# Opening loads in halves with the constants last, and low parts one step later in the selecting attention

## The chip, the cores and the metric

The kernel runs on one core of one Trainium2 chip. The metric is the device time of an execution in microseconds (us), lower is better. Engines: PE (TensorE, matrix products), DVE (VectorE), ACT (ScalarE), POOL (GpSimd), SP (SyncE, here only a DMA queue).

## The reference, cut to what matters

Two transformer-like blocks over 512 tokens of width 1024, all in float32. The first block runs twice (two layers), the second once. Each layer begins with `h = rms_norm(x, g)` and a wide projection `z = h @ w_in`. The first block then mixes multi-head latent attention, a two-dimensional Fourier transform of `h` (`fourier_mix`) and windowed attention; rotary angles come from `positions`. The second block mixes a linear recurrence, a pooling branch and a *selecting* attention (`dsa_attention`: an index score picks 128 keys per query out of up to 512, and eight heads attend to those alone); later it attends to a memory of 256 vectors, whose keys and values (`m @ w_kv`) are independent of the tokens.

## The kernel before, in words

**Operands in two parts.** Each float32 operand of a matrix product is split into a rounded high part (`hi`, written by ACT as fp32r) and the remainder (`lo = value - hi`, by DVE or POOL). A product takes three matmuls: hi·hi, hi·lo, lo·hi (lines 672 to 677).

**The weight stream.** All weights lie in one tensor `stream` in the order of their use, cut into units of 128 x 2048 floats (1 MiB, 16 blocks of 128 x 128). SP loads unit v into `raw[v % 2]` (line 650 for unit 0, 654 for unit 1, 658 for all others) as soon as the low part of unit v-2 is done (semaphore `lo_ready`). ACT writes `w_hi` once PE has finished with the unit two before (`split_unit`, line 1315); DVE writes `w_lo` (line 1953; by halves in `split_piece`, line 2177), which counts up `lo_ready`; PE waits for it before the first block of a unit.

**The start (layer 0).** SP issues unit 0, then x in four transfers of 512 KB (two of eight row groups each), then unit 1. ACT's queue issues the gain vector `g_in`, `pos_i` (positions) and `cst_sb` (identity, ones, masks, frequencies). ACT splits unit 0 (line 1647), then for each of the eight row groups m of x writes `raw_x_hi[m]` (1651) and its square (1652). DVE writes `w_lo[0]` (2420) and then the eight `raw_x_lo[m]` (2424), adds up the squares (2428, 2429), and splits units 2 and 3 (1953). PE (`begin`) takes unit 0 over k = 0..7, six matmuls of 512 columns for each k, then unit 1. Within unit 1, at n = 0 and k = 5, it sums the squares over the partitions (`begun_sum`, line 800, against the ones in `cst_sb`); from this ACT makes the reciprocal root, DVE the normed x (`res`, lines 2023 and 2447), ACT its high part `h_hi` (1367), and POOL its low part `h_lo` (2782).

**POOL's order.** POOL waits for `pos_loaded` and `cst_loaded`, runs `turns()` (lines 2870 to 2879: thirteen instructions, a cast, nine tensor_scalar, three tensor_tensor, each waiting for the one before), which makes the reduced rotary angles `cs`, and only behind them the eight `h_lo` of the layer. Nothing reads `cs` before some 70 us. The Fourier stage `four1`, which follows `begin` on PE, waits for `h_lo` of k = 0 and 1 before its first tile.

**The selecting attention** (`attention(c, "dsa", ...)`). 32 items t (a head and a block of 128 queries). DVE, in step t: the masked minimum of the scores of item t (2199, "reduce", counts `shift_ready`); at t = 11, 19, 27 the low part of a finished output (`output_lo`, 2229); reciprocal and scaling of item t-1 (2212, 2214); then `evac_mem(t)`, which holds the low parts of the weight units. PE, in step t: for even t the score matmuls of t and t+1 (883), which wait for the reduce of t-1; the transposes of item t-3 (908); the value products (957); then two blocks of the memory's keys (up to t = 15) or one of its values (t = 16 to 31). ACT's steps hold exponentials (1510), copies (1499) and, at fixed t, the `w_hi` of units. The unit whose low part is written at t = 5 and 6 ("am"'s last split) is the second of the memory's keys; PE needs it in step 8.

Of the kernel before, what the change touches and what calls it, by code (L numbers as in the profile page):

```python
# [14 lines left out]
P = 128  # L15
# [248 lines left out]
def block_kernel(nc, stream, xT, pT, memT, vec1, gains, cst, pos, out):  # L264
    with ExitStack() as ctx:
        def sem(name):
            return ctx.enter_context(nc.semaphore(name))
# [151 lines left out]

        def home(c, v):  # L420

            block = 1 if c.base is BASE1 else 2
            wrapped = block == 1 and v >= TOTAL1["U"]
            if wrapped:
                v -= TOTAL1["U"]
            if block == 1 and c.layer == 0 and v < 2 and not wrapped:
                return second if v == 1 else (w_hi[0], w_lo[0])
            for (b, st), two in EARLY.items():
                u = v - c.base[st]["U"] if b == block else -1
                if 0 <= u < 2 and two[u] is not None:  # L430
                    return two[u]
            return w_hi[v % 2], w_lo[v % 2]
# [27 lines left out]
        tile_free = sem("tile_free")  # L460
        x_loaded = [sem(f"x_loaded{i}") for i in range(4)]
# [186 lines left out]
        @block.sync  # L648
        def _(sp):
            sp.dma_start(raw[0][:, :], stream[0]).then_inc(raw_ready[0], 16)  # L650
            for i in range(4):
                k = slice(2 * i, 2 * i + 2)
                sp.dma_start(x[:, k, :], xT.rearrange("(k p) s -> p k s", p=P)[:, k, :]).then_inc(x_loaded[i], 16)
            sp.dma_start(raw[1][:, :], stream[1]).then_inc(raw_ready[1], 16)
            with sp.Fori(1, UNITS_PADDED // 2) as i:
                for p in range(2):
                    sp.wait_ge(lo_ready, i * 2 + (p - 1))
                    sp.dma_start(raw[p][:, :], stream[bass.ds(i * 2 + p, 1)].rearrange("a p n -> (a p) n")).then_inc(raw_ready[p], 16)
            for p in range(2):
                sp.wait_ge(raw_ready[p], 16 * (UNITS_PADDED // 2))  # L660
# [3 lines left out]
        def _(pe):  # L664
# [159 lines left out]
            def begin(c, st, turn):  # L824

                u0 = c.base[st]["U"]
                if turn == 0:
                    pe.wait_ge(lo_ready, c.at("U", st, 1))
                    hi, lo = home(c, u0)
                    two = [free_bank(c, st, n) for n in range(2)]  # L830
                    for k in range(KD):
                        pe.wait_ge(raw_split, c.begun("W", 2 * k + 2))
# [7 lines left out]
                    for n in range(2):  # L840
                        ps = free_bank(c, st, 2 + n)
                        for k in range(KD):
                            b = slice((8 * n + k) * P, (8 * n + k + 1) * P)
                            mm = mac_at(ps[:, :], hi[:, b], lo[:, b], raw_x_hi[:, k, :], raw_x_lo[:, k, :], k == 0, k == KD - 1)
                            if n == 0 and k == 5:
                                begun_sum(c, 0, 0)
                                begun_sum(c, 1, 0)
# [442 lines left out]
        def _(act):  # L1290
# [353 lines left out]
            act.dma_start(pos_i[:, :], pos).then_inc(pos_loaded, 16)  # L1644
            act.dma_start(cst_sb[:, :], cst).then_inc(cst_loaded, 16)
            act.wait_ge(raw_ready[0], 16)
            nc.scalar.activation(w_hi[0][:, :], raw[0][:, :], ACT.Copy).then_inc(hi_ready, 1)
            act.wait_ge(gain_loaded, 16)
            for m in range(KD):
                act.wait_ge(x_loaded[m // 2], 16)  # L1650
                nc.scalar.activation(raw_x_hi[:, m, :], x[:, m, :], ACT.Identity, scale=g_in[:, m:m + 1]).then_inc(raw_hi, 2)
                nc.scalar.activation(sq_x[:, m, :], x[:, m, :], ACT.Square).then_inc(x_squared, 1)
            act.wait_ge(raw_ready[1], 16)
            nc.scalar.activation(second[0][:, :], raw[1][:, :], ACT.Copy).then_inc(hi_ready, 1)
            log_table()
# [277 lines left out]
        def _(dve):  # L1933
# [487 lines left out]
            first_low(0, w_hi[0], w_lo[0])  # L2421
            for m in range(KD):
                dve.wait_ge(raw_hi, 2 * m + 2)
# [326 lines left out]
            def evac_mem(t):  # L2750
                if t in (5, 6):
                    split_piece(c, "am", SPLIT_LATER["am"], t - 5)
                after_blocks(c, "mk", t, 2, lambda n: None)
                if t in (25, 33):
                    split_unit(c, "mv", (t - 25) // 8)
# [443 lines left out]
```

## Time and profile before

| | us |
|---|---|
| median of 3 runs | 2708.15 (2705.16 to 2709.49) |
| the profiled execution | 2703.69 |
| its span, first to last instruction | 2701.7 |

The profiled execution is 2.0 us longer than its span, and 4.5 us below the median. A change of about 0.2% (5.4 us) can be told from none. The page gives, by engine, the busy share; by line, count, duration and the idle time ahead. A busy PE counts matmuls whose ends are modelled, so only its idle gaps and its rate tell something.

### The profile page before, as it was taken

How to read it: one execution, taken by the hardware profiler on the slowest of the kernel's cores; microseconds unless marked ns; L12 is line 12 of the kernel's file. 1: busy time of each engine (PE TensorE's matmuls, PEld its weight loads, DVE VectorE, ACT ScalarE, POOL GpSimd, SP SyncE). 2: the span in 40 equal slices, each digit the busy share in tenths (PEclk: the TensorE clock that was granted, in tenths of full speed). 3: DMA queues.
4: the chain of work that ended last, by engine and by line, in shares of the span. 5: the costliest groups of instructions: out<-in, count | busy, mean ns of one | idle time of the engine just before them, and what ended most of it. 6: DMA issues, size and time to landing. Idle time of an engine off the chain costs nothing. (4 is left out here: it accounts for less than half of the span.)

```text
span 2701.7 us, 40494 instructions
## 1 busy us (share of the span) xinstructions
PE 2633.5 (97%) x15788; PEld 2264.9 (84%) x15788; DVE 1711.3 (63%) x2738; ACT 1303.0 (48%) x2274; POOL 558.3 (21%) x556
## 2 busy tenths in 40 slices
PE   8999999999999999999999999999999999999997
PEld 6887778999888988777899998897787688899976
DVE  6667544888624765754388862466688537698733
ACT  6446543555524643654355552463634535555521
POOL 5124001210402312400121031241001012210131
PEclk9999999999999999999999999999999999999999
DMA  4321123222332232111222232222232222123332
GB/s 151 125 94 40 48 78 110 78 93 96 110 109 97 85 116 94 48 56 63 101 87 94 102 118 94 95 94 94 78 123 80 79 94 79 48 94 107 106 112 83
DMA packets 37558, 246.55 MB, mean 91 GB/s; under 512 B 4608, under 2 KB 5632, under 8 KB 8448
## 3 DMA queue, kind: packets, MB, share of 16 engines
q1 hardware_dynamic: 33632, 239.09, 24.9%
q10 hardware_dynamic: 3744, 4.94, 0.5%
q8 instruction: 126, 2.06, 0.3%
q14 instruction: 56, 0.46, 0.1%
HBM read 241.91 MB, written 2.10 MB: 90 GB/s over the span
## 5 line engine op out<-in xcount | busy, mean ns | idle before, releaser
L1953 DVE TENSOR_TENSOR w_lo<-raw,w_hi 128x2048 fp32r<-128x2048 f32 x130 | 305.4, 2351 | 320.3 <-ACT w_hi L1315 319.8
L675 PE MATMUL bank<-h_hi,w_hi 128*128 128x512 f32 (+1 forms) x1224 | 472.3, 386 | 3.2 <-DVE ob_lo L2464 1.3
L677 PE MATMUL bank<-h_hi,w_lo 128*128 128x512 f32 (+1 forms) x1224 | 463.7, 379 | 0.0
L676 PE MATMUL bank<-h_lo,w_hi 128*128 128x512 f32 (+1 forms) x1224 | 463.3, 378 | 0.0
L1315 ACT ACTIVATE w_hi<-raw 128x2048 fp32r<-128x2048 f32 x151 | 288.1, 1910 | 240.0 <-PE bank L677 231.3
L1065 PE MATMUL bank<-half_hi,w_hi 128*128 128x256 f32 x1344 | 380.5, 283 | 0.0
L1066 PE MATMUL bank<-half_lo,w_hi 128*128 128x256 f32 x1344 | 380.4, 283 | 0.0
L1067 PE MATMUL bank<-half_hi,w_lo 128*128 128x256 f32 x1344 | 380.3, 283 | 0.0
L675 PEld LDWEIGHTS bank<-h_hi,w_hi 128*128 128x128 f32 x1224 | 230.3, 188 | 55.4 <-issue 11.5
L677 PEld LDWEIGHTS bank<-h_hi,w_lo 128*128 128x128 f32 x1224 | 230.2, 188 | 44.2
L676 PEld LDWEIGHTS bank<-h_lo,w_hi 128*128 128x128 f32 x1224 | 230.6, 188 | 39.7
L1065 PEld LDWEIGHTS bank<-half_hi,w_hi 128*128 128x128 f32 x1344 | 257.9, 192 | 0.3
L1066 PEld LDWEIGHTS bank<-half_lo,w_hi 128*128 128x128 f32 x1344 | 258.0, 192 | 0.1
L1067 PEld LDWEIGHTS bank<-half_hi,w_lo 128*128 128x128 f32 x1344 | 258.0, 192 | 0.0
L675 PE MATMUL bank<-a_hi,w_hi 128*128 128x512 f32 x528 | 206.8, 392 | 6.6 <-POOL a_lo L2809 5.8
L676 PE MATMUL bank<-a_lo,w_hi 128*128 128x512 f32 x528 | 206.2, 390 | 0.0
L677 PE MATMUL bank<-a_hi,w_lo 128*128 128x512 f32 x528 | 206.0, 390 | 0.0
L2300 DVE TENSOR_TENSOR w_lo<-raw,w_hi 128x512 fp32r<-128x512 f32 x192 | 141.0, 736 | 32.6 <-ACT w_hi L1558 31.4
L1499 ACT ACTIVATE pT<-bank 128x512 f32<-128x512 f32 (+3 forms) x168 | 83.0, 494 | 127.6 <-PE bank L908 125.1
L1558 ACT ACTIVATE w_hi<-raw 128x512 fp32r<-128x512 f32 x192 | 118.7, 623 | 18.0 <-PE bank L1067 9.7
L675 PEld LDWEIGHTS bank<-a_hi,w_hi 128*128 128x128 f32 x528 | 99.4, 188 | 29.1 <-POOL a_lo L2809 7.0
L2782 POOL TENSOR_TENSOR m_lo<-res,m_hi 128x512 fp32r<-128x512 f32 x24 | 31.1, 1294 | 436.8 <-ACT m_hi L1367 436.8
(508 smaller groups left out, 5802.9 us busy)
## 6 DMA issues: line engine op xcount, KB each, us to landing
raw<-in_stream SPq DMA_DIRECT2D x226, 1024.0 KB, 4.8
x<-in_xT SPq DMA_DIRECT2D x4, 512.0 KB, 8.7
out_T<-x ACTq DMA_DIRECT2D x8, 256.0 KB, 2.0
p_f<-in_pT ACTq DMA_DIRECT2D x2, 512.0 KB, 3.6
memf<-in_memT ACTq DMA_DIRECT2D x1, 1024.0 KB, 5.4
cst_sb<-in_cst ACTq DMA_DIRECT2D x1, 409.0 KB, 7.3
pos_i<-in_pos ACTq DMA_DIRECT2D x1, 258.0 KB, 6.1
g_in<-in_gains ACTq DMA_DIRECT2D x3, 4.0 KB, 3.5
```

What stands on the lines that cost most here:

```text
L675: nc.tensor.matmul(ps, wh, xh, start=start, stop=False)
L676: nc.tensor.matmul(ps, wh, xl, start=False, stop=False)
L677: return nc.tensor.matmul(ps, wl, xh, start=False, stop=stop)
L1065: nc.tensor.matmul(ps, wh[:, b], half_hi[:, i, k, :], start=opens, stop=False, skip_group_check=on)
L1066: nc.tensor.matmul(ps, wh[:, b], half_lo[:, i, k, :], start=False, stop=False, skip_group_check=on)
L1067: mm = nc.tensor.matmul(ps, wl[:, b], half_hi[:, i, k, :], start=False, stop=k == KD // 2 - 1, skip_group_check=on)
L1315: nc.scalar.activation(home(c, v)[0][:, :], raw[v % 2][:, :], ACT.Copy).then_inc(hi_ready, 1)
L1499: nc.scalar.activation(a["pT"][h % 2][:, 0:n, b * P:(b + 1) * P], TURNED[:, 0:n * P].rearrange("p (t q) -> p t q", t=n), ACT.Copy).then_in ...
L1558: ins = nc.scalar.activation(factor(c, v, i, w_hi), factor_value(c, v, i), ACT.Copy)
L1953: nc.vector.tensor_tensor(lo[:, :], raw[v % 2][:, :], hi[:, :].bitcast(F32), ALU.subtract).then_inc(lo_ready, 1)
L2300: ins = nc.vector.tensor_tensor(factor(c, v, i, w_lo), factor_value(c, v, i), factor(c, v, i, w_hi).bitcast(F32), ALU.subtract)
L2782: nc.gpsimd.tensor_tensor(dst, src, hi.bitcast(F32), ALU.subtract).then_inc(res_split, 1)
```

## The change

Four edits at the start and one in the selecting attention:

- Unit 0 comes in two halves by k (k = 0..3 and 4..7 of both of its column tiles, pieces of 2 KB in a row): half 0, x's first transfer, half 1, x's other three, unit 1. `cst` and `pos` move from ACT's queue to the end of SP's opening list, behind unit 1.
- ACT and DVE split half 0 first, then m = 0 of x, then half 1; PE waits for half 0 only and for `lo_ready` at k = 4. The squares of x come one or more steps later on ACT, the last four behind unit 1's high part.
- The sum of squares moves on PE from k = 5 to k = 7 of unit 1's first tile.
- In the selecting attention DVE writes the low parts in halves at t = 6, 7 (was 5, 6), 10, 11 and 18, 19 (were 9, 10 and 17, 18), 26, 27 and 33, 34 (were whole units at 25 and 33). ACT's and PE's orders there stay.

```diff
@@ -417,6 +417,10 @@
             (2, "gu"): [early("gu2_0", 0, 8), early("gu2_1", 16, 24)],
         }
 
+        def of_front(w, half):
+
+            return w.rearrange("p (n k c) -> p n (k c)", n=2, k=KD)[:, :, half * (KD // 2) * P:(half + 1) * (KD // 2) * P]
+
         def home(c, v):
 
             block = 1 if c.base is BASE1 else 2
@@ -458,6 +462,9 @@
         part_done = sem("part_done")
         act_took = sem("act_took")
         tile_free = sem("tile_free")
+        front_loaded = sem("front_loaded")
+        front_hi = sem("front_hi")
+        front_split = sem("front_split")
         x_loaded = [sem(f"x_loaded{i}") for i in range(4)]
         gain_loaded = sem("gain_loaded")
         post_ready = sem("post_ready")
@@ -647,11 +654,15 @@
 
         @block.sync
         def _(sp):
-            sp.dma_start(raw[0][:, :], stream[0]).then_inc(raw_ready[0], 16)
+            sp.dma_start(of_front(raw[0], 0), of_front(stream[0], 0)).then_inc(front_loaded, 16)
             for i in range(4):
                 k = slice(2 * i, 2 * i + 2)
                 sp.dma_start(x[:, k, :], xT.rearrange("(k p) s -> p k s", p=P)[:, k, :]).then_inc(x_loaded[i], 16)
+                if i == 0:
+                    sp.dma_start(of_front(raw[0], 1), of_front(stream[0], 1)).then_inc(raw_ready[0], 16)
             sp.dma_start(raw[1][:, :], stream[1]).then_inc(raw_ready[1], 16)
+            sp.dma_start(cst_sb[:, :], cst).then_inc(cst_loaded, 16)
+            sp.dma_start(pos_i[:, :], pos).then_inc(pos_loaded, 16)
             with sp.Fori(1, UNITS_PADDED // 2) as i:
                 for p in range(2):
                     sp.wait_ge(lo_ready, i * 2 + (p - 1))
@@ -825,10 +836,12 @@
 
                 u0 = c.base[st]["U"]
                 if turn == 0:
-                    pe.wait_ge(lo_ready, c.at("U", st, 1))
+                    pe.wait_ge(front_split, 1)
                     hi, lo = home(c, u0)
                     two = [free_bank(c, st, n) for n in range(2)]
                     for k in range(KD):
+                        if k == KD // 2:
+                            pe.wait_ge(lo_ready, c.at("U", st, 1))
                         pe.wait_ge(raw_split, c.begun("W", 2 * k + 2))
                         for n in range(2):
                             b = slice((8 * n + k) * P, (8 * n + k + 1) * P)
@@ -842,7 +855,7 @@
                         for k in range(KD):
                             b = slice((8 * n + k) * P, (8 * n + k + 1) * P)
                             mm = mac_at(ps[:, :], hi[:, b], lo[:, b], raw_x_hi[:, k, :], raw_x_lo[:, k, :], k == 0, k == KD - 1)
-                            if n == 0 and k == 5:
+                            if n == 0 and k == 7:
                                 begun_sum(c, 0, 0)
                                 begun_sum(c, 1, 0)
                         mm.then_inc(tile_done, 1)
@@ -1641,17 +1654,24 @@
                 act.dma_start(g_in[:, :], gains[bass.ds(row, 1)].rearrange("a p n -> (a p) n")).then_inc(gain_loaded, 16)
 
             act.dma_start(g_in[:, :], gains[0]).then_inc(gain_loaded, 16)
-            act.dma_start(pos_i[:, :], pos).then_inc(pos_loaded, 16)
-            act.dma_start(cst_sb[:, :], cst).then_inc(cst_loaded, 16)
-            act.wait_ge(raw_ready[0], 16)
-            nc.scalar.activation(w_hi[0][:, :], raw[0][:, :], ACT.Copy).then_inc(hi_ready, 1)
+            act.wait_ge(front_loaded, 16)
+            nc.scalar.activation(of_front(w_hi[0], 0), of_front(raw[0], 0), ACT.Copy).then_inc(front_hi, 1)
             act.wait_ge(gain_loaded, 16)
+
+            def square_x(m):
+                nc.scalar.activation(sq_x[:, m, :], x[:, m, :], ACT.Square).then_inc(x_squared, 1)
             for m in range(KD):
                 act.wait_ge(x_loaded[m // 2], 16)
                 nc.scalar.activation(raw_x_hi[:, m, :], x[:, m, :], ACT.Identity, scale=g_in[:, m:m + 1]).then_inc(raw_hi, 2)
-                nc.scalar.activation(sq_x[:, m, :], x[:, m, :], ACT.Square).then_inc(x_squared, 1)
+                if m == 0:
+                    act.wait_ge(raw_ready[0], 16)
+                    nc.scalar.activation(of_front(w_hi[0], 1), of_front(raw[0], 1), ACT.Copy).then_inc(hi_ready, 1)
+                elif m <= 4:
+                    square_x(m - 1)
             act.wait_ge(raw_ready[1], 16)
             nc.scalar.activation(second[0][:, :], raw[1][:, :], ACT.Copy).then_inc(hi_ready, 1)
+            for m in range(4, KD):
+                square_x(m)
             log_table()
             act.wait_ge(tile_done, Counts(BASE1, 0).at("T", "z1a", 2))
             for u in range(2):
@@ -2418,8 +2438,12 @@
             def first_low(v, hi, lo):
                 dve.wait_ge(hi_ready, v + 1)
                 nc.vector.tensor_tensor(lo[:, :], raw[v][:, :], hi[:, :].bitcast(F32), ALU.subtract).then_inc(lo_ready, 1)
-            first_low(0, w_hi[0], w_lo[0])
+            dve.wait_ge(front_hi, 1)
+            nc.vector.tensor_tensor(of_front(w_lo[0], 0), of_front(raw[0], 0), of_front(w_hi[0], 0).bitcast(F32), ALU.subtract).then_inc(front_split, 1)
             for m in range(KD):
+                if m == 1:
+                    dve.wait_ge(hi_ready, 1)
+                    nc.vector.tensor_tensor(of_front(w_lo[0], 1), of_front(raw[0], 1), of_front(w_hi[0], 1).bitcast(F32), ALU.subtract).then_inc(lo_ready, 1)
                 dve.wait_ge(raw_hi, 2 * m + 2)
                 nc.vector.scalar_tensor_tensor(out=raw_x_lo[:, m, :], in0=x[:, m, :], scalar=g_in[:, m:m + 1],
                                                in1=raw_x_hi[:, m, :].bitcast(F32), op0=ALU.mult, op1=ALU.subtract).then_inc(raw_split, 2)
@@ -2748,11 +2772,14 @@
             dve.wait_ge(res_ready, result_value(c, "normm", KD - 1))
 
             def evac_mem(t):
-                if t in (5, 6):
-                    split_piece(c, "am", SPLIT_LATER["am"], t - 5)
-                after_blocks(c, "mk", t, 2, lambda n: None)
-                if t in (25, 33):
-                    split_unit(c, "mv", (t - 25) // 8)
+                if t in (6, 7):
+                    split_piece(c, "am", SPLIT_LATER["am"], t - 6)
+                for u in range(2):
+                    if t in (8 * u + 10, 8 * u + 11):
+                        split_piece(c, "mk", u, t - 8 * u - 10)
+                for u in range(2):
+                    if t in (7 * u + 26, 7 * u + 27):
+                        split_piece(c, "mv", u, t - 7 * u - 26)
             attention(c, "dsa", lambda h, b: (score[:, b, 0:(b + 1) * P], 1.0), also=evac_mem)
             merge(c, 2, "cm", 2)
             project_norm(c, "wout", "post1", 2, "mix_post", "normh")
```

## Rows read from the trace of the kernel before

**Rows 1.** The page's part 1: busy time of each engine
```profile
PE 2633.5 (97%) x15788; PEld 2264.9 (84%) x15788; DVE 1711.3 (63%) x2738; ACT 1303.0 (48%) x2274; POOL 558.3 (21%) x556
```

**Rows 2.** Waits of PE, whole execution: total, times, longest
```profile
PE bank L675 <- DVE raw_x_lo L2424: 11.1, 1, 11.1
```

**Rows 3.** Timeline of the start: start us, us, what [idle before <-releaser]
```profile
5.72 1.91 ACT L1647 ACTIVATE w_hi<-raw 128x2048 fp32r<-128x2048 f32 x1 [2.25 <-DMA raw<-in_stream]
7.67 2.29 DVE L2420 TENSOR_TENSOR w_lo<-raw,w_hi 128x2048 fp32r<-128x2048 f32 x1 [7.67 <-ACT w_hi L1647]
...
9.88 5.86 DVE L2424 SCALAR_TENSOR_TENSOR raw_x_lo<-x,g_in,raw_x_hi 128x512 fp32r<-128x512 f32 x6
...
11.12 0.77 PE L675 MATMUL bank<-raw_x_hi,w_hi 128*128 128x512 f32 x1 [11.12 <-DVE raw_x_lo L2424]
...
16.38 0.42 PE L675 MATMUL bank<-raw_x_hi,w_hi 128*128 128x512 f32 x1
```

**Rows 4.** DMA issues to landing: page part 6; then tile raw, 0 to 40
```profile
cst_sb<-in_cst ACTq DMA_DIRECT2D x1, 409.0 KB, 7.3
pos_i<-in_pos ACTq DMA_DIRECT2D x1, 258.0 KB, 6.1
...
DMA to landing us min/median/max: 4.8/4.9/11.6
```

**Rows 5.** Timeline of POOL, 0 to 80 us
```profile
9.14 1.29 POOL L2870 CAST posf<-pos_i 128x516 f32<-128x516 int32 x1 [8.69 <-DMA cst_sb<-in_cst]
...
17.17 1.49 POOL L2876 TENSOR_SCALAR ang<-ang 64x512 f32<-64x512 f32 x1
18.75 1.29 POOL L2877 TENSOR_TENSOR ang<-ang,ang 64x512 f32<-64x512 f32 x1
...
26.05 2.35 POOL L2876 TENSOR_SCALAR ang<-ang 64x512 f32<-64x512 f32 x1
...
30.89 3.92 POOL L2878 TENSOR_SCALAR ang<-ang,cst_sb 64x512 f32<-64x512 f32 x1
...
36.56 7.54 POOL L2782 TENSOR_TENSOR h_lo<-res,h_hi 128x512 fp32r<-128x512 f32 x6 [0.18 <-POOL cs L2879]
```

**Rows 6.** Timeline of DVE, 19 to 70 us
```profile
24.91 2.13 DVE L2429 TENSOR_TENSOR sq_x<-sq_x 128x1024 f32<-128x1024 f32 x1
26.97 5.97 DVE L1953 TENSOR_TENSOR w_lo<-raw,w_hi 128x2048 fp32r<-128x2048 f32 x2
```

**Rows 7.** Timeline of PE where the Fourier stage begins
```profile
37.99 0.37 PE L672 MATMUL bank<-w_hi,h_hi 128*128 128x288 f32 x1 [0.63 <-POOL h_lo L2782]
...
39.13 0.40 PE L672 MATMUL bank<-w_hi,h_hi 128*128 128x288 f32 x1 [0.51 <-POOL h_lo L2782]
```

**Rows 8.** Timeline of PE, selecting attention: six pairs of score matmuls
```profile
2075.68 0.70 PE L883 MATMUL bank<-kk,qd 64*128 64x256 f32 x4 [1.06 <-DVE st_neg L2199]
...
2087.42 0.49 PE L883 MATMUL bank<-kk,qd 64*128 64x128 f32 x4 [1.76 <-DVE st_neg L2199]
...
2092.75 0.70 PE L883 MATMUL bank<-kk,qd 64*128 64x256 f32 x4
...
2104.30 0.49 PE L883 MATMUL bank<-kk,qd 64*128 64x128 f32 x4
...
2108.19 0.70 PE L883 MATMUL bank<-kk,qd 64*128 64x256 f32 x4
...
2115.74 1.13 PE L883 MATMUL bank<-kk,qd 64*128 64x512 f32 x4
```

**Rows 9.** Windows, same stage: stretch, busy by engine, PEclk, DMA, GB/s
```profile
2088.00:2092.00 4.00, 4.00 (x26) 3.39 (x26) 2.14 (x9) 3.79 (x9) 0.00 (x0) 0.57 0.62 248
```

**Rows 10.** Timeline of DVE in the same stage
```profile
2083.26 1.23 DVE L2177 TENSOR_TENSOR w_lo<-raw,w_hi 128x1024 fp32r<-128x1024 f32 x1 [2.25 <-ACT w_hi L1315]
...
2112.87 0.69 DVE L2229 TENSOR_TENSOR od_lo<-bank,od_hi 128x512 fp32r<-128x512 f32 x1 [1.15 <-ACT od_hi L1537]
...
2114.87 0.55 DVE L2199 CUSTOM_DVE_ANT_0 prob<-score,bank 128x384 f32<-128x384 f32 x1
```

## The prediction

> **What bounds the kernel now.** The page's part 1 comes first: PE holds matmuls for 2633.5 of the span's 2701.7 us [rows 1]. So PE is the bound, and a change is worth what it takes out of PE's idle gaps and slow stretches, or adds to them. The view of PE's waits shows which gaps there are: the longest by far is the first, 11.1 us for the first `raw_x_lo` [rows 2]. The timeline of the start shows the chain into it: unit 0 lands at 5.7, ACT splits it (1.91 us), DVE writes its low part (2.29 us), then the first `raw_x_lo`, and PE starts at 11.12 [rows 3]. Its first twelve matmuls take until 16.38, 0.44 us each, the pace of the 1.2 GHz level [rows 3].
>
> The reader should then look past the start for the next thing PE waits for. That is at 37.99 and 39.13: PE enters the Fourier stage 0.63 and 0.51 us late, each time for an `h_lo` of POOL [rows 7]. POOL's timeline says why: the thirteen instructions of `turns()` run from 9.14 to 36.38, and the first `h_lo` starts behind them at 36.56 [rows 5]. POOL is only 21% busy over the span [rows 1], and yet it is the bound just here. The start that the change shortens therefore ends in a stage that POOL gates already.
>
> In the selecting attention the one long gap is at 2087.42: 1.76 us for a reduce of DVE [rows 8], which stood behind the first half of a low part that had itself waited 2.25 us for ACT [rows 10]. Right after it the granted clock averages 0.57 over 4 us, thus mostly the 1.2 GHz level [rows 9].
>
> **The start, part by part.** Half 0 has half the bytes; ACT's and DVE's instructions on it take about half (DVE needs 1.23 us for 128x1024 elsewhere [rows 10]). Half 0 should land near 4.3, ACT end at 5.3, DVE at 6.5; x's first transfer lands about 5.6, `raw_x_hi[0]` ends at 6.6, `raw_x_lo[0]` at 7.4, and PE starts at 7.5, 3.6 us sooner. Half 1 (7.0) is split by 9.4 and `raw_x_lo[1]` done at 10.1, which is when PE, with six slow matmuls at 0.44 us, comes to k = 1. ACT's new wait for half 1 holds `raw_x_hi[1]` to `[7]` back by some 0.5 us, DVE's for its high part `raw_x_lo[1]`; neither reaches PE. After that DVE's 0.98 us per row group [rows 3] is faster than PE's six matmuls. The deferred squares cost nothing: ACT finishes them near 18.5, DVE's two sums near 23.3, and PE's sum of squares, moved two k later, comes at 26.2. PE leaves unit 1 at 33.6 instead of 37.2. This cover is 2.9 us thick.
>
> Now the price. Five megabytes go out at the opening, whatever their order. Unit 1, last of the 4.87 MB to land, is there at 3.5 + 11.6 = 15.1; `pos_i` and `cst_sb` land at 7.3 and 9.0 today [rows 4]. Put behind unit 1 on the same queue, they take its place: 15.1, so POOL starts `turns()` at 15.3 instead of 9.14 [rows 5]. (SP's list has one transfer more and the two constants, some 0.5 us of issue each, all issued before the first wait for `lo_ready`; nothing else stands behind them.)
>
> How long `turns()` takes then is the unknown. The trace before shows a rule: a POOL instruction that begins while DVE is inside an instruction with two SBUF inputs takes as long as that one still lasts, and its own time on top. The tensor_scalar at 26.05 lasts 2.35, because the sum of squares runs until 27.04; the one at 30.89 lasts 3.92, because `w_lo` runs until 32.94 [rows 5, 6]. Own times are 1.49 for a tensor_scalar and 1.29 for a tensor_tensor, read where DVE was idle [rows 5], and 1.87 for the one at 30.89. In the other direction DVE is stretched less: two `w_lo` in 5.97 instead of 4.58 [rows 6, 3]. With this I lay out the new order. From 15.3, cast and one tensor_scalar until 17.4. Then DVE's `second_lo`, two sums and two `w_lo` run back to back from 16.5 to 28.6, and POOL gets one instruction in behind each: ends at 19.9, 23.1, 24.7, 27.3, 29.8. That is seven of thirteen. DVE's next instructions read PSUM and do not hold POOL up, as the last at 34.89 (1.49) and `h_lo` at 1.26 each [rows 5] show. The other six take 3 x 1.49 + 2 x 1.29 + 1.87 and 0.1 between each: 9.4. `turns()` ends at about 39.1, against 36.4: **+2.7**. The six us of delay shrink because POOL spent the old early time mostly locked out by the `raw_x_lo`. PE reaches the Fourier stage at 33.6 and starts it at 40.7: the 3.6 us won are gone and 2.7 are lost on top.
>
> Bounds: if DVE never held POOL up, thirteen instructions would end near 34.7, PE would start at 36.3, -1.7. If `turns()` took its 27.2 us again [rows 5], it would end at 42.5, +6.1. The laid-out order is nearest to how the rows behave, so I take it.
>
> What is late next is the clock. PE idles 7 us, and the attention shows that a gap of 1.76 us can be enough to drop it [rows 8, 9]. Its price there: score pair to score pair takes 5.33 us after the gap (2087.42 to 2092.75) and 3.89 for the same work eight items later (2104.30 to 2108.19) [rows 8], 1.4 us. Here the first tile waits for `h_lo` twice anyway, so I take **+1.0**; bounds 0 and 2.6 (half of the 5.26 us that the slow stretch at the start lasts [rows 3]).
>
> Of this a page of the Trainium skill says more. By "SBUF — State Buffer", section "Who interferes with whom", the lock is exclusive both ways: who issues first keeps it for a whole instruction, and the other fully blocks. Then DVE's instructions too would wait for the whole of POOL's, `turns()` would end near 42.6 and the total be about 3.5 us worse than mine. The rows agree for POOL waiting for DVE; for DVE waiting for POOL they do not (a `w_lo` issued at 26.97 against a POOL instruction of about 1.4 us is not late by that much), so I keep the stretch that the rows show.
>
> **The selecting attention.** Moving the halves to t = 6 and 7 puts the reduce of 6 ahead of the wait for ACT. Laid out from DVE's rows, reduce 7 ends at 2085.5 instead of 2087.3, and PE goes on without a gap: 1.76 won. But the second half now ends at 2087.2, and PE needs it for the keys in step 8, which it would reach at 2086.3: a new wait of 0.95, which leaves 0.85. A gap of 1.06 us before item 2 [rows 8] was followed by full pace, so the slow stretch should go as well: 1.4 more. Together **-2.3** by item 10.
>
> Then it gives back. Each later unit's second half now falls in t = 11, 19 and 27, the very steps with `output_lo`. There DVE has little slack: reduce 21 ends at 2115.42 and PE wants it at 2115.74, behind an `output_lo` at 2112.87 [rows 8, 10]. One more 1.14 us (its slot) ahead of reduce 20, less 0.4 that the earlier steps run ahead, makes PE wait 0.6. The same layout gives 0.57 and 0.6 at 11 and 27: **+1.8**. The pieces at 33 and 34 lie in the drain, behind the last scaling: nothing. Net **-0.5**. Bounds: -3.2 (gap and slow stretch gone, collisions free), +0.9 (slow stretch stays).
>
> **Sum.** +2.7 + 1.0 - 0.5 = +3.2 on the profiled execution's 2703.7: 2706.9. Its runs' median stands 4.5 higher, so the forecast for the median is 2708.15 + 3.2 = 2711.3.
>
> **The rivals.** (A) The forecast, POOL late by about 3 us: 0.50. (B) The lock blocks both ways or the constants land later, `turns()` ends at 42 to 43: +6.2 + 1.4 - 0.5, median 2715.3, clearly slower. For it: several big DVE instructions of the start are stretched already. Against: only by part of a POOL instruction. 0.15. (C) The other side, faster: the gain at the start reaches the end. Its place is `turns()`'s end; it decides if that lies before 32.2, when PE, leaving unit 1 at 33.6, never waits. Then -3.6, and with an attention free of collisions -3.2: 2701.4. For it: POOL's work alone is short. Against: even unblocked it ends near 34.7. 0.10. (D) POOL ends about where it did, because the early lock-outs are worth more than I count; PE starts the Fourier stage as before, the reheating of 1.0 and -0.5 to -2.5 stay: 2707.5. 0.20. (E) A as to the start, while the clock still drops in the attention and all three collisions bite: +0.9 instead of -0.5, 2712.7. 0.05. That a part has no effect is not among them: each edit moves instructions of its own.
>
> **How the numbers follow.** Within 0.2% (5.4 us, about what a measurement tells from none) lie most of A, D and E and a little of B and C: 0.66. Slower by more: B's bulk and A's upper end, 0.24. Faster by more: C, 0.10. The range of 8 in 10 leaves out C and B's far end: 2705 to 2717.
>
> **What would show it.** PE's first matmul near 7.5; POOL's cast near 15.3 and `cs` near 39; PE idle some 7 us ahead of line 672, put down to `h_lo`, and the granted clock at half behind it; in the attention no gap for `st_neg` before item 8, a wait of about 1 us for `w_lo` of line 2177 behind it, and three of about 0.6 for `st_neg` at items 14, 22, 30. Wrong it would be if the constants land well before 14, if `turns()` takes under 20 us, or if PE's wait for `h_lo` is under 4 us.

## The result, and the profile after

The changed kernel takes 2714.45 us in the median of 14 runs (2711.54 to 2716.24), the kernel before 2707.35 in 14 beside them: a ratio of 1.0025, 95% interval 1.0017 to 1.0033, thus slower by 6.8 us (4.6 to 8.9). The profiled execution took 2713.32, its span is 2711.2. A second set of ten runs gave 1.0024 (1.0015 to 1.0033).

From PE's waits in the changed kernel (waited for; us in total, times, longest), the two longest single ones:

```profile
PE bank L683 <- POOL h_lo L2809: 10.1, 3, 9.1
PE bank L686 <- DVE raw_x_lo L2448: 9.5, 1, 9.5
```

The first wait, 11.1 before [rows 2], is 9.5. The one for `h_lo`, 0.63 before [rows 7], is 9.1. Both ends of the start are in PE's timeline, and between them lies the gap:

```profile
9.50 0.77 PE L686 MATMUL bank<-raw_x_hi,w_hi 128*128 128x512 f32 x1 [9.50 <-DVE raw_x_lo L2448]
...
34.37 0.39 PE L688 MATMUL bank<-raw_x_hi,second_lo 128*128 128x512 f32 x1
43.83 0.58 PE L683 MATMUL bank<-w_hi,h_hi 128*128 128x288 f32 x1 [9.07 <-POOL h_lo L2809]
```

POOL's timeline says what it waited for (before: [rows 5]):

```profile
17.00 0.88 POOL L2897 CAST posf<-pos_i 128x516 f32<-128x516 int32 x1 [16.55 <-DMA pos_i<-in_pos]
...
19.65 3.84 POOL L2899 TENSOR_SCALAR ang<-ang,cst_sb 64x512 f32<-64x512 f32 x1
...
28.61 2.75 POOL L2903 TENSOR_SCALAR ang<-ang 64x512 f32<-64x512 f32 x1
31.44 1.30 POOL L2904 TENSOR_TENSOR ang<-ang,ang 64x512 f32<-64x512 f32 x1
...
40.75 1.49 POOL L2906 TENSOR_SCALAR cs<-ang 64x512 f32<-64x512 f32 x1
42.42 7.44 POOL L2809 TENSOR_TENSOR h_lo<-res,h_hi 128x512 fp32r<-128x512 f32 x6 [0.18 <-POOL cs L2906]
```

`turns()` begins at 17.00 (before 9.14), takes 25.2 us (before 27.2) and ends at 42.24 (before 36.38): PE comes 5.84 us late into the Fourier stage. The longest of POOL's instructions, the one at 19.65, stands through two of DVE's:

```profile
18.29 2.52 DVE L2440 TENSOR_TENSOR second_lo<-raw,second_hi 128x2048 fp32r<-128x2048 f32 x1 [0.89 <-ACT second_hi L1672]
20.73 2.28 DVE L2452 TENSOR_TENSOR sq_x<-sq_x 128x2048 f32<-128x2048 f32 x1
```

From within the gap on the clock is at half for ten microseconds (about 40 to 50), as PE's windows of 4 us show (busy time and instructions of PE, granted clock, DMA share, GB/s):

```profile
34.00:38.00 4.00, 0.76 (x4) 1.00 0.14 57
38.00:42.00 4.00, 0.00 (x0) 0.74 0.00 0
42.00:46.00 4.00, 2.09 (x7) 0.50 0.01 2
46.00:50.00 4.00, 4.00 (x19) 0.50 0.00 0
```

In the window of 46 to 50 PE issues 19 matmuls where the kernel before issued 29. By 54.35, where PE resumes behind `U_lo` (the low part of the stage's first product), for which it waited at 46.18 before, it is 8.17 us behind: 5.84 for POOL and 2.33 for the clock.

Why the start won 1.6 instead of 3.6 us is in ACT's timeline. Half 0 is there no sooner than the whole unit was (5.7 [rows 3]), and x's first part comes behind it at 7.77:

```profile
5.89 1.06 ACT L1658 ACTIVATE w_hi<-raw 128x1024 fp32r<-128x1024 f32 x1 [3.44 <-DMA raw<-in_stream]
7.77 0.72 ACT L1665 ACTIVATE raw_x_hi<-x,g_in 128x512 fp32r<-128x512 f32 x1 [0.82 <-DMA x<-in_xT]
9.01 1.06 ACT L1668 ACTIVATE w_hi<-raw 128x1024 fp32r<-128x1024 f32 x1 [0.52 <-DMA raw<-in_stream]
```

The DMA view of 1 to 7 us gives for the kernel before, and then for the changed one:

```profile
DMA packets 651, 1.78 MB, mean 297 GB/s; under 512 B 176, under 2 KB 176, under 8 KB 523
```

```profile
DMA packets 765, 1.22 MB, mean 203 GB/s; under 512 B 172, under 2 KB 172, under 8 KB 765
```

More packets, and a third fewer bytes: in the changed kernel none reaches 8 KB, since a half is cut into rows of 2 KB (x's rows have 2 KB in both kernels).

In the selecting attention the 1.76 us gap ahead of item 8 [rows 8] is gone and the clock stays at 1.00 there. Four waits are left between 2083 and 2145 us, beside the one of 1.06 at item 2, which both have:

```profile
2097.96 0.36 PE L686 MATMUL bank<-mem_hi,w_hi 128*128 128x256 f32 x1 [0.79 <-DVE w_lo L2197]
...
2108.91 1.13 PE L896 MATMUL bank<-kk,qd 64*128 64x512 f32 x4 [0.32 <-DVE st_neg L2219]
2124.74 1.13 PE L896 MATMUL bank<-kk,qd 64*128 64x512 f32 x4 [0.32 <-DVE st_neg L2219]
2140.58 1.13 PE L896 MATMUL bank<-kk,qd 64*128 64x512 f32 x4 [0.37 <-DVE st_neg L2219]
```

PE enters this attention 10.60 us behind the kernel before (first score pair at 2083.10 against 2072.50), is 8.24 behind after item 9, and 9.44 at 2140.58: the attention wins 2.36 and gives 1.20 back, net -1.16.

One piece is neither start nor attention: from 8.17 behind at 54 us to 10.60 at 2083, although no edit lies between. The experiments turn to it under "before_again".

### The profile page after: what moved, and what is told of

It reads as the page before. It is cut to its first block and busy times, and to the rows that moved or that the text cites. A ratio compares the mean times of both kernels' runs of the same rounds, so it can differ in the third digit from the quotient of the medians.

```text
span 2711.2 us, 40500 instructions
## 1 busy us (share of the span) xinstructions
PE 2636.3 (97%) x15788; PEld 2267.2 (84%) x15788; DVE 1709.3 (63%) x2741; ACT 1302.6 (48%) x2275; POOL 554.8 (20%) x556
```

## The experiments

Theory P: the end of `turns()` on POOL sets when PE enters the Fourier stage, whatever PE's start, and the idle gap costs clock on top. The rivals are named with each run. So many us behind (or sooner) means, where nothing else is named, by how much the same instruction comes later (or sooner) than in the first profile of the kernel before.

**attn_only** is the kernel before with the attention's edit alone.

```diff
-                if t in (5, 6):
-                    split_piece(c, "am", SPLIT_LATER["am"], t - 5)
-                after_blocks(c, "mk", t, 2, lambda n: None)
-                if t in (25, 33):
-                    split_unit(c, "mv", (t - 25) // 8)
+                if t in (6, 7):
+                    split_piece(c, "am", SPLIT_LATER["am"], t - 6)
...
```

> The kernel before with the selecting attention's edit alone; the start is untouched. Theory P (the loss is POOL's late turns() and the clock behind it, all of it at the start): the start looks as before (PE from 11.1, Fourier stage entered at 38.0), the attention has no gap for the reduce before item 8, a wait of about 0.8 for w_lo and three of 0.3 to 0.4 at items 14, 22 and 30, 1.2 us less by its end, and the time is 1 us below the kernel before, or the same within what can be told. Rival W (the loss comes from the attention's new waits): 3 us or more above the kernel before. Rival K (drops of the granted clock that hang on no edit): a half-clock stretch can come or go at 235, 378, 1122, 1267 or 1618 us even here, about 1.2 us each.

Measured: 2708.16 against 2707.72, ratio 1.0003 (0.9994 to 1.0012). Rival W falls. Its waits are those of the changed kernel: 0.80 for `w_lo`, then 0.32, 0.34 and 0.37. In the trace the attention wins 1.14 us (PE is 2.59 behind when it begins and 1.45 at item 30), which is too little for the interval to show.

**start_only** is the changed kernel with the old attention (the same edit, the other way).

> The changed kernel with the selecting attention as it was before. Theory P: PE enters the Fourier stage at 43.8 as in the changed kernel, is 8 us behind the kernel before by the end of that stage, and the time is 7 to 9 us above the kernel before. Rival W: as fast as the kernel before within 2 us. Rival K: half-clock stretches besides the one at 40 to 50 us move the time by 1.2 us each, in either direction.

Measured: 2716.22, ratio 1.0032 (1.0020 to 1.0044), 8.7 us slower; PE enters the Fourier stage at 43.91 behind a gap of 9.23. The whole loss is the start's, within the intervals.

**const_last** is the kernel before with the constants moved and nothing else.

```diff
             sp.dma_start(raw[1][:, :], stream[1]).then_inc(raw_ready[1], 16)
+            sp.dma_start(cst_sb[:, :], cst).then_inc(cst_loaded, 16)
+            sp.dma_start(pos_i[:, :], pos).then_inc(pos_loaded, 16)
...
-            act.dma_start(pos_i[:, :], pos).then_inc(pos_loaded, 16)
-            act.dma_start(cst_sb[:, :], cst).then_inc(cst_loaded, 16)
```

> The kernel before with one edit: the two constants behind unit 1 on SP's queue. No halves. Theory P: they land at about 16.5, turns() ends at 41 to 43, PE leaves unit 1 at 37.2 as before, waits 4 to 6 us for h_lo and pays 1 to 2.4 us of clock; 6 to 8 us above the kernel before, thus as slow as the whole change although it wins nothing at the start. Rival H (the halves and the new order of ACT and DVE do the harm): within 2 us of the kernel before.

Measured: 2713.24, ratio 1.0022 (1.0013 to 1.0030), 6.0 us slower. This one edit holds nearly the whole loss. POOL's first and third instruction and PE's entry:

```profile
15.52 1.17 POOL L2870 CAST posf<-pos_i 128x516 f32<-128x516 int32 x1 [15.06 <-DMA pos_i<-in_pos]
...
18.89 4.94 POOL L2872 TENSOR_SCALAR ang<-ang,cst_sb 64x512 f32<-64x512 f32 x1
```

```profile
45.01 0.58 PE L674 MATMUL bank<-w_hi,h_hi 128*128 128x288 f32 x1 [8.11 <-POOL h_lo L2782]
```

The constants come 1.5 us sooner than in the changed kernel and `turns()` still ends 1.2 us later (43.42): the third instruction begins together with `second_lo` and stands through it and the first sum (4.94 for 3.84), and the fifth stands behind a `w_lo` (3.56 for 2.51). Where PE resumes behind `U_lo` (54.73 against 46.18) it is 8.55 us behind; the changed kernel is 8.17 behind there in one profile and 7.71 in the other. The halves at the start thus won less than 1 us that lasted.

**const_act** is the changed kernel with the two constants back on ACT's queue (the edit above, undone).

> The changed kernel with one edit taken back: the two constants on ACT's queue behind the first gains, as before. Theory P: they land by 10, turns() starts near 9.5 and ends at 36 to 37, PE leaves unit 1 near 34.8 and enters the Fourier stage at 37 to 38.5, so that the start is worth nothing or up to 1 us; the time is within 2 us of the kernel before and 5 to 9 us under the changed one. Rival H: it stays 5 us or more above the kernel before. Rival L (the lock holds DVE up as fully as POOL): early constants make the chain raw_x_lo of DVE late, PE waits for raw_x_lo(2) and on, and leaves unit 1 only at 36 or later.

Measured: 2707.22, ratio 1.0001 (0.9993 to 1.0010). The loss is gone; rival H falls. But the start missed what I expected: PE starts at 11.31 and leaves unit 1 at 37.46, not 34.8, and enters the next stage at 38.32. With constants in flight beside the 2 KB rows (1.28 MB by 7 us), x's first part comes at 9.37:

```profile
6.55 1.06 ACT L1658 ACTIVATE w_hi<-raw 128x1024 fp32r<-128x1024 f32 x1 [3.13 <-DMA raw<-in_stream]
9.37 0.72 ACT L1665 ACTIVATE raw_x_hi<-x,g_in 128x512 fp32r<-128x512 f32 x1 [1.76 <-DMA x<-in_xT]
```

A busy POOL also slows DVE's `raw_x_lo` (2.43 us for the last three, against 2.08 in the changed kernel with POOL idle), a part of rival L. It never makes PE wait again after its first matmul, so what sets its start is x's landing. The 1.6 us that the changed kernel won at its start were therefore bought with the constants' delay.

**pe_kept_busy** fills PE's gap in the changed kernel; the products are overwritten.

```diff
                     ps = free_bank(c, "four1", n)
+                    if L == 0 and n == 0:
+                        for _ in range(36):
+                            nc.tensor.matmul(ps[:, :], w_hi[u][:, 0:P], raw_x_hi[:, 0, :], start=True, stop=True)
```

> The changed kernel, with 36 idle matmuls (128x512, their product is overwritten) on PE in the gap before the first h_lo, about 8.2 us of work in a gap of 9.07. POOL's work and its end at 42.2 are untouched. Theory P with its clock term (an idle PE costs the clock, not the gap itself): no half-clock stretch from 40 to 50 us, PE enters the Fourier stage at 43.8 as before and leaves it 2.3 us sooner, the time is 2.3 us below the changed kernel, or 2710 to 2713. Rival N (the slow matmuls of that stage come from waits on POOL's later h_lo or on U_lo): nothing is won, and the stage takes as long at a full clock.

Measured: 2715.88, ratio 1.0028 (1.0017 to 1.0040). In the trace the clock term is as said:

```profile
46.00:50.00 4.00, 4.00 (x32) 1.00 0.01 2
741.00:745.00 4.00, 4.00 (x12) 0.57 0.53 223
2151.00:2155.00 4.00, 4.00 (x23) 0.61 0.57 180
2595.00:2599.00 4.00, 4.00 (x13) 0.64 0.46 195
```

32 matmuls from 46 to 50 instead of 19, entry at 43.96, and the sum behind the stage starts at 61.80 instead of 63.92: 2.1 us sooner, rival N falls. In the time nothing of it shows. Against the first profile of the changed kernel the same instructions stay 2.1 us sooner until 479 us, where PE waits 0.9 for ACT's `sq` as it does not there. Then three short half-clock stretches follow (the last three rows) that neither profile of the changed kernel has, 1.5 to 1.6 us each, and it ends 4.5 us later. Stretches stand at nearly the same places in runs whose PE did rest at the start: const_act has one at 732, halves_joined has them at 2152 and 2596. So they need no start without rest; whether one makes them more likely, one profile can't say. That keeping PE busy locally restores the clock is shown; that it pays is not.

**halves_joined** lays unit 0 out so that a half is one row of 4 KB per partition.

```diff
-            return w.rearrange("p (n k c) -> p n (k c)", n=2, k=KD)[:, :, half * (KD // 2) * P:(half + 1) * (KD // 2) * P]
+            return w[:, half * UC // 2:(half + 1) * UC // 2]
...
+            stream[0] = stream[0].reshape(P, 2, 2, UC // 4).transpose(0, 2, 1, 3).reshape(P, UC).copy()
```

> The changed kernel with the columns of unit 0 laid out so that each half is one run of 4 KB in a partition's row instead of two of 2 KB. Theory S (transfers in 2 KB pieces ran at 180 to 250 GB/s instead of 400, and this is why half 0 landed at 5.9): half 0 lands at 4.3 to 4.8, raw_x_lo(0) is done and PE starts at 8 to 8.6 instead of 9.5. POOL still starts at 16 to 17 and PE still enters the Fourier stage at 43 to 44, so the time is that of the changed kernel within 1.5 us. Rival Q (it is x's first transfer, or queueing of all of them, whatever the size of the pieces): half 0 lands at 5.7 to 6 again.

Measured: 2714.24, ratio 1.0015 (1.0006 to 1.0024); the median is the changed kernel's. From 1 to 7 us 1.62 MB instead of 1.22:

```profile
DMA packets 722, 1.62 MB, mean 270 GB/s; under 512 B 185, under 2 KB 185, under 8 KB 722
```

Its ACT and PE, from their timelines:

```profile
5.17 1.06 ACT L1659 ACTIVATE w_hi<-raw 128x1024 fp32r<-128x1024 f32 x1 [2.69 <-DMA raw<-in_stream]
6.50 0.72 ACT L1666 ACTIVATE raw_x_hi<-x,g_in 128x512 fp32r<-128x512 f32 x1 [0.28 <-DMA x<-in_xT]
```

```profile
8.29 0.77 PE L686 MATMUL bank<-raw_x_hi,w_hi 128*128 128x512 f32 x1 [8.29 <-DVE raw_x_lo L2449]
42.66 0.58 PE L683 MATMUL bank<-w_hi,h_hi 128*128 128x288 f32 x1 [8.99 <-POOL h_lo L2810]
```

PE starts 1.2 us sooner than in the changed kernel, as theory S said, though half 0 lands at 5.2 and not at 4.3 to 4.8. So the size of the rows is a large part of why the halves came late, not all. By the Trainium skill's page "DMA: Bandwidth & Descriptors", section "Why small descriptors are slow (HBM only)", a packet costs a fixed overhead of some three cycles beside its beats of 32 bytes, which for 2 KB would be about 5%, an estimate from the page. Over 1 to 7 us the rows here show far more: 203 against 270 GB/s between rows of 2 and of 4 KB. It is no rate of 2 KB rows as such, though. From 7 to 10 us the kernel before and then the changed one move only packets under 8 KB, x's rows of 2 KB among them, and both at full pace:

```profile
DMA packets 576, 1.22 MB, mean 407 GB/s; under 512 B 48, under 2 KB 48, under 8 KB 576
```

```profile
DMA packets 636, 1.22 MB, mean 407 GB/s; under 512 B 40, under 2 KB 40, under 8 KB 636
```

Short rows are slow in the first microseconds alone (217 GB/s in the changed kernel at 3 to 4 us, where the kernel before has 411); why, no run shows. And PE waits for POOL all the same, nearly as long.

**whole_load** is const_act with unit 0 loaded in one transfer and only split by halves.

```diff
-            sp.dma_start(of_front(raw[0], 0), of_front(stream[0], 0)).then_inc(front_loaded, 16)
+            sp.dma_start(raw[0][:, :], stream[0]).then_inc(raw_ready[0], 16)
...
```

> The run const_act (constants early on ACT's queue) with unit 0 loaded whole and only split by halves. Theory S: unit 0 lands at 5.7 and x's first part by 7, half 0 is split by 8.0, PE starts near 9.0 to 9.5 instead of 11.3. POOL's turns() ends at 36 to 37, so PE, out of unit 1 by 34.5 to 35, still enters the Fourier stage at 38, and the time is that of the kernel before within 2 us; a gap of 3 us may cost up to 1 us of clock. Rival Q: PE starts at 11 again.

Measured: 2708.53, ratio 1.0002 (0.9992 to 1.0011). The time came out as said, the start did not: unit 0 is there at 6.04, x's first part only at 8.74 behind it, and PE starts at 10.69. `turns()` ends at 36.53, PE enters the stage at 38.13, behind a gap of 1.46. Half a clock follows that gap (0.67 over 40 to 44 us), so PE is 1.67 behind where it resumes behind `U_lo` (47.85), and only 0.14 of it is the entry. const_act, with a gap of 0.86 at the same place, keeps its full clock. Here the start was again worth nothing.

**best1** adds three edits to whole_load, two of them on POOL.

```diff
-                link(nc.gpsimd.tensor_scalar(b, b, ROUND, None, ALU.add))
-                link(nc.gpsimd.tensor_scalar(b, b, -ROUND, None, ALU.add))
+                link(nc.gpsimd.tensor_scalar(b, b, ROUND, -ROUND, ALU.add, ALU.add))
...
                 link(nc.gpsimd.tensor_copy(posf[:, :], pos_i[:, :]))
+                pool.wait_ge(cst_loaded, 16)
...
-            pool.wait_ge(cst_loaded, 16)
...
-                for u in range(2):
-                    if t in (8 * u + 10, 8 * u + 11):
-                        split_piece(c, "mk", u, t - 8 * u - 10)
...
+                after_blocks(c, "mk", t, 2, lambda n: None)
```

> whole_load with three more edits: POOL's two additions of the rounding constant in one instruction (12 instead of 13), its first conversion no longer waiting for the constants, and in the selecting attention the low part of unit am at steps 6 and 7 with the later units where they were before. Theory P (the end of turns() sets when PE enters the Fourier stage): turns() ends at 32 to 33.5, PE enters the stage at 35 to 35.5, and the attention is worth 1.8 to 2.4 without the three new waits; together 3 to 5 us below the kernel before (2703 to 2705). If PE is held by something else, h_hi or the sum of squares, it enters at 37 or later and only the attention's part is won.

Measured: 2703.95, ratio 0.9984 (0.9975 to 0.9993): 4.3 us faster than the kernel before. The attention brings 2.4 in the trace (PE is 1.18 behind at its first score pair and 1.18 ahead at item 10). PE enters the stage at 36.68, 1.3 sooner than before, but not at 35, because the time saved on POOL was lost again against DVE:

```profile
27.45 6.04 POOL L2898 TENSOR_SCALAR ang<-ang,cst_sb 64x512 f32<-64x512 f32 x1
```

```profile
26.11 5.60 DVE L1969 TENSOR_TENSOR w_lo<-raw,w_hi 128x2048 fp32r<-128x2048 f32 x2
```

POOL's instruction began inside the first `w_lo` and did not get in between the two: it ended 1.8 us after the second, its own time. The Trainium skill's page "SBUF — State Buffer", section "Who interferes with whom", says that a DVE instruction with two SBUF inputs contends with a GpSimd instruction that reads SBUF, and the trace agrees. That the other fully blocks for a whole instruction, which the prediction took for these too, it says where it speaks of DVE's 2-port modes; of back-to-back instructions it says nothing.

Not every POOL instruction is kept out. In the traces of all these runs each one of `turns()` that stood through two of DVE's low parts or sums of squares reads a column of `cst_sb` as well (line 2899 in the changed kernel, 2872 in const_last, 2898 here). Those without `cst_sb` that began inside the same blocks got in at the seam. In the kernel before this one begins inside the first `w_lo` of the same pair, which ends at 29.66, and is done long before the second, which ends at 32.94:

```profile
28.48 2.31 POOL L2877 TENSOR_TENSOR ang<-ang,ang 64x512 f32<-64x512 f32 x1
```

Whether the read of `cst_sb` is the reason no run tests.

**before_again** is the kernel before, for a second profile.

> The kernel before, unchanged, for a second profile. Theory G (each kernel has some short half-clock stretches past the start, at places where PE rests a little, and how many fall in one execution is chance; the first profile had 3 of them besides the end): this one shows 4 to 7, at 227, 370, 1113, 1257, 1618, 2142 or 2585 us, and is up to 4 us longer than the first. Rival (they belong to the kernel): the same three, at 1112, 1617 and 2088 us.

Measured: profiled 2709.85 us, span 2707.9, against 2701.7 the first time. PE's windows of the first profile, then of the second:

```profile
1112.00:1116.00 4.00, 4.00 (x25) 0.57 0.24 45
1258.00:1262.00 4.00, 4.00 (x19) 1.00 0.56 236
1617.00:1621.00 4.00, 4.00 (x12) 0.57 0.60 242
2088.00:2092.00 4.00, 4.00 (x26) 0.57 0.62 248
2142.00:2146.00 4.00, 4.00 (x20) 1.00 0.62 252
```

```profile
371.00:375.00 4.00, 3.86 (x16) 0.58 0.31 90
1115.00:1119.00 4.00, 4.00 (x25) 0.57 0.09 14
1258.00:1262.00 4.00, 3.52 (x16) 0.57 0.21 39
1617.00:1621.00 4.00, 2.44 (x11) 1.00 0.00 0
2091.00:2095.00 4.00, 4.00 (x29) 0.57 0.75 262
2142.00:2146.00 4.00, 3.05 (x21) 0.56 0.22 45
2146.00:2150.00 4.00, 4.00 (x11) 0.59 0.53 221
```

Theory G holds: of the same kernel's half-clock stretches some stand in both profiles (at 1112 or 1115, and at 2088 or 2091), some in one alone. Over one, PE loses 1.2 to 1.6 us. The second profile, against the first, is 2.3 us behind after the stretch at 40 us, falls from 2.44 to 3.67 at 370, from 3.71 to 5.08 at 1258 and by 2.8 over the two at 2142 to 2150, and gains 1.6 at 1617, where only the first has one. These steps add up to 6.1 of the 6.2 us between the two spans. The first profile had few stretches, which fits its place 4.5 us under the median. The 2.4 us between start and attention above are mostly of this kind: the changed kernel's profile has stretches at 234, 377 and 1265 us that the first profile of the kernel before lacks (1.2, 1.3 and 1.4) and lacks the one at 1617 (-1.6).

**after_again** is the changed kernel once more.

> The changed kernel, unchanged, for a tighter ratio and a second profile. Front: PE starts at 9.5, turns() ends at 42.2, the Fourier stage is entered at 43.8, one half-clock stretch of some 10 us there. Theory G: the short stretches behind it (4 in the first profile) fall elsewhere or in another number. Time 2713 to 2716, ratio 1.002 to 1.003; the run with PE kept busy had 1.0028, so if this one is again at 1.0025 or below, keeping the clock up at the start is not worth its 2.1 us in the end.

Measured: 2714.01, ratio 1.0024 (1.0015 to 1.0033); PE enters the stage at 43.88, the stretch at 234 of the first profile is missing, and those at 377, 1121 and 1265 are there again. So POOL's part repeats to 0.1 us; the stretches keep to few places, and which of them one execution has varies.

**best2** lets the last two of POOL's steps follow the `h_lo` of layer 0.

```diff
-                a, b, d = ang[0][r, :], ang[1][r, :], ang[2][r, :]
+                a, b, d = cs[r, :], ang[1][r, :], ang[2][r, :]
...
                 norm_begun(c)
+                if L == 0:
+                    turns_end()
```

> best1 with the angle kept in cs, so that the last two of POOL's steps can follow the h_lo of layer 0 (cs is wanted at 72 us). In best1 the last but one stood 6.04 us behind DVE's two w_lo. Theory P: POOL has done its ten steps by 27.4, h_lo(0) starts as soon as h_hi is there, 32.6 to 33.2, PE goes from unit 1 into the Fourier stage without a gap over 0.3 us at 35.9 to 36.1, 0.7 us sooner than best1: 2702 to 2704. Rival H2 (h_hi or DVE's res becomes the bound, held up by POOL's h_lo): a gap of 0.5 us or more again.

Measured: 2703.39 in the median of 12 runs, eleven of them between 2698.48 and 2705.04; ratio 0.9980 (0.9971 to 0.9989). One run took 5244.98 us, which nothing here explains. POOL has done its ten steps at 27.37 and waits for work, PE has no wait for `h_lo` left:

```profile
26.08 1.29 POOL L2897 TENSOR_TENSOR cs<-cs,ang 64x512 f32<-64x512 f32 x1
34.01 7.55 POOL L2802 TENSOR_TENSOR h_lo<-res,h_hi 128x512 fp32r<-128x512 f32 x6 [6.63 <-ACT h_hi L1375]
```

PE enters the stage at 36.29, 1.7 us sooner than before. Rival H2 falls.

**best3** puts the same POOL steps behind joined halves, with the constants on SP between x and unit 1.

```diff
+            sp.dma_start(pos_i[:, :], pos).then_inc(pos_loaded, 16)
+            sp.dma_start(cst_sb[:, :], cst).then_inc(cst_loaded, 16)
             sp.dma_start(raw[1][:, :], stream[1]).then_inc(raw_ready[1], 16)
-            sp.dma_start(cst_sb[:, :], cst).then_inc(cst_loaded, 16)
-            sp.dma_start(pos_i[:, :], pos).then_inc(pos_loaded, 16)
```

> best2's POOL steps and attention with the changed kernel's start: halves of unit 0 as joined 4 KB rows, constants on SP's queue, but behind x and ahead of unit 1. Theory P: half 0 lands at 4.5 to 5.2, PE starts at 8.3 and leaves unit 1 at 33.7 to 34; constants land at 12 to 14, the ten steps of turns() are done by 31 to 33, unit 1 lands at 15.5 to 16.5 and its low part is there before PE wants it at 21.5; PE enters the Fourier stage at 34 to 35: 2 us below best2, 2700 to 2702. If unit 1 now comes late, PE waits for it at 21 us; if DVE's block of instructions from 17 to 29 shuts POOL out, the stage is entered at 36 or later and it is no better than best2.

Measured: 2701.97, ratio 0.9980 (0.9971 to 0.9989), 5.4 us faster than the kernel before, and by the medians 12 us under the changed one. PE starts at 8.43 and unit 1 does not come late, but the stage is entered at 35.37, behind a wait of 0.56 for `h_lo`, since POOL's ten steps ran until 33.85 beside DVE's block. It is not told apart from best2.

## Why the prediction was right or wrong

The time lies in the range (2705 to 2717), on its upper side: 3.2 us above the forecast of 2711.3, and beside the 2715.3 of rival B. The way was right and the size was not: +6.8 us measured against +3.2 forecast. That the time itself is off by only 3.2 is in part luck, since the median of the kernel before came out 0.8 lower in 14 runs than in the 3 of the forecast. Slower by more than 0.2% had a chance of 0.24, within 0.2% one of 0.66; the ratio of 1.0025 is the former, with an interval (from 1.0017) that reaches into the latter. By its steps:

- **PE starts at 7.5.** Measured 9.50. The step that failed is "Half 0 should land near 4.3": it was 5.9, and x's first part behind it 7.8 instead of 5.6. The opening moved rows of 2 KB at 203 GB/s. PE's late start cost nothing in the end, because the gain was unused either way.
- **PE leaves unit 1 at 33.6.** Measured 34.76, 1.2 late where the start was 2.0 late: PE's slow stretch at the start lasted 3.1 us (9.50 to 12.63) and not 5.3.
- **Constants land at 15.1, POOL starts at 15.3.** Measured 17.00, 1.7 us of the miss. It is the halves' slow opening: with unit 0 whole (const_last) POOL starts at 15.52, with rows of 4 KB (halves_joined) at 16.06.
- **`turns()` takes 23.8 us.** Measured 25.2, 1.4 us of the miss. The rule that POOL stands until DVE's two-input instruction is over, and its own time on top, held within 0.2 us for the three instructions behind the first sum. What failed is "POOL gets one instruction in behind each": DVE's `second_lo` and first sum ran back to back from 18.29 to 23.01, and line 2899, which reads `cst_sb`, stood through both (3.84 us). +2.7 became +5.84.
- **Reheating +1.0, bounds 0 to 2.6.** Measured +2.33. I priced it by the slow stretch behind a 1.76 us gap; behind 9 us at rest PE had half a clock from about 40 to 50, of which it was at work for six. The nearer row was the start of the kernel, the prediction's own upper bound.
- **The attention -0.5.** Measured -1.16. The first part came out as laid out (-2.36 for -2.3, the wait for `w_lo` 0.79 for 0.95). The collisions are where they were put, at items 14, 22 and 30, and smaller: 0.32, 0.32 and 0.37 for 0.6 each.
- **The sum.** 5.84 + 2.33 - 1.16 = +7.0, against +6.8 by the ratio and +3.2 forecast. The spans of the two profiles differ by 9.5; the other 2.5 are half-clock stretches in the main, which the prediction's sum leaves out.

Rival B had the size, by one of its two ways: "the constants land later", and `turns()` ended at 42.2. Its other way, a lock that blocks DVE for the whole of POOL's instruction, isn't in the traces: `second_lo` took 2.52 with POOL at work against 2.29 for a DVE instruction of that form alone [rows 3]. Rival C needed POOL done before 32.2; only best2, with two steps moved behind, comes there (27.4). Rival D needed `turns()` to end near 36 again; begun 7.9 us later and only 2 us shorter, it ended at 42. What was right is the mechanism: POOL gates the stage behind the start, so PE's gain is lost and POOL's delay passes on. const_last and const_act show it, and best2 shows the gate open once POOL's steps are out of the way.

One premise deserves a mark: the sum was made against one profiled execution. A second profile of the same kernel is 6.2 us longer in the span; 2.3 of that are there where PE resumes behind `U_lo` (48.47 against 46.18): it enters the stage 0.8 later, behind a gap of 1.28, and has half a clock there too. So the changed kernel is 8.2 us behind the one profile and 5.9 behind the other at this point.

## What to carry to other kernels

Before you speed up a stage, look at what gates the next one: here POOL's chain of thirteen small steps took its inputs from two transfers, 0.7 MB together, that looked harmless to move, and shortening or moving that chain brought what the faster start could not. When you cut a transfer at the opening of a kernel, don't take half the bytes for half the time: here halves in rows of 2 KB landed no sooner than the whole. Where two instructions of DVE with two SBUF inputs run back to back, a POOL instruction can stand through both; here this hit only those that read a column of constants from SBUF too. And before you build on one profile, take a second: here they differed by as much as the change.

## What was not expected of the hardware

- Rows of 2 KB instead of longer ones took the opening transfers from 297 to 203 GB/s over 1 to 7 us; rows of 4 KB gave 270. From 7 to 10 us both kernels move packets under 8 KB at 407.
- A POOL instruction of 1.8 us that reads `cst_sb` took 6.04 behind two DVE instructions in a row, with no opening at the seam; others, without `cst_sb`, got in there.
- Two profiles of one kernel differ by 6 us of 2702, nearly all of it lost at half-clock stretches, 1.2 to 1.6 us each, that come in one execution and not in the other. What decides whether one comes is open.
